# Turning the gated activation of both feed-forward networks on TensorE instead of on VectorE and ScalarE

## The reference, cut to what matters

```python
# first block
h2 = _rmsnorm(x, ffn_norm_w[l])
g, u = jnp.split(jnp.einsum('bsd,df->bsf', h2, w_gate_up[l]), 2, axis=-1)
x = x + jnp.einsum('bsf,fd->bsd', jax.nn.silu(g) * u, w_down[l])
# second block
h2 = _rms(x, g_norm2) * (1 + sc2) + sh2
gate, up = jnp.split(h2 @ w_ffn_in, 2, axis=-1)
x = x + gt2 * ((jax.nn.silu(gate) * up) @ w_ffn_out)
```

## Time and profile before

| | us |
|---|---|
| median of three runs (lowest, highest) | 2671.17 (2670.88, 2673.14) |
| the profiled execution, its own time | 2671.17 |
| its span in the trace | 2669.1 |
| TensorE busy, matmuls | 2629.4 |
| VectorE busy | 1775.1 |
| ScalarE busy | 1425.9 |

### The profile page before, as it was taken

How to read it: one execution, slowest core, us unless ns; L and a number is a source line. 1 busy time by engine, 2 the same in 40 slices (tenths; PEclk the granted TensorE clock), 3 DMA queues, 4 the chain that set the end, 5 groups by cost and what they waited for, 6 DMA issues and landing times.

```text
span 2669.1 us, 34070 instructions
## 1 busy us (share of the span) xinstructions
PE 2629.4 (99%) x12229; PEld 2188.9 (82%) x12229; DVE 1775.1 (67%) x2082; ACT 1425.9 (53%) x1844; POOL 3.2 (0%) x9
## 2 busy tenths in 40 slices
PE   8999999999999999999899999999999999999999
PEld 6888888778888888888788888888788888887887
DVE  5788677577777777888776554566577645445565
ACT  5555554456565655445556565644455555565443
POOL 0000000000000000000000000000000000000000
PEclk9999999999999999999999999999999999999999
DMA  7766555678888888888565455565578766666655
GB/s 256 241 202 197 158 143 158 214 242 278 290 276 290 276 290 271 302 281 274 175 214 179 152 166 174 152 220 187 180 248 291 250 192 191 194 189 191 203 189 173
DMA packets 306487, 583.54 MB, mean 219 GB/s; under 512 B 24095, under 2 KB 24441, under 8 KB 305865
## 3 DMA queue, kind: packets, MB, share of 16 engines
q1 hardware_dynamic: 305328, 578.45, 67.3%
q10 hardware_dynamic: 744, 2.27, 0.2%
q0 software_dynamic: 304, 1.33, 0.2%
HBM read 579.86 MB, written 2.11 MB: 218 GB/s over the span
## 4 chain that ended last, share of the span: by engine, by line
PE 92%; DVE 4%; ACT 2%; DMA 1%; issue 1%; SPq 0%; ACTq 0%; DVEq 0%
PE acc L344 29%; PE acc L346 29%; PE acc L345 29%; DVE lo L333 2%; PE ex L1031 1%; PE aux L1052 1%; PE aux L588 1%; ACT hi L327 1%; DMA raw<-w_ffn_out 1%; DMA raw<-w_proj_mla 0%; DVE op_lo L506 0%; ACT stage L491 0%; PE tp L531 0%; DVE op_hi L505 0%; PE tp L1013 0%
## 5 line engine op out<-in xcount | busy, mean ns | idle before, releaser
L333 DVE TENSOR_TENSOR lo<-raw,hi 128x1024 fp32r<-128x1024 f32 x895 | 1078.7, 1223 | 498.6 <-ACT hi L327 477.6
L327 ACT ACTIVATE hi<-raw 128x1024 fp32r<-128x1024 f32 x895 | 928.8, 1056 | 531.5 <-PE acc L346 382.7
L344 PE MATMUL acc<-hi,op_hi 128*128 128x512 f32 x2752 | 1087.5, 395 | 14.5 <-DVE lo L333 10.3
L346 PE MATMUL acc<-hi,op_lo 128*128 128x512 f32 x2752 | 1074.7, 391 | 0.0
L345 PE MATMUL acc<-lo,op_hi 128*128 128x512 f32 x2752 | 1074.1, 390 | 0.0
L344 PEld LDWEIGHTS acc<-hi,op_hi 128*128 128x128 f32 x2752 | 518.5, 188 | 126.9 <-issue 18.4
L346 PEld LDWEIGHTS acc<-hi,op_lo 128*128 128x128 f32 x2752 | 518.2, 188 | 109.6
L345 PEld LDWEIGHTS acc<-lo,op_hi 128*128 128x128 f32 x2752 | 518.9, 189 | 103.2
L344 PE MATMUL acc<-hi,f_hi 128*128 128x512 f32 x704 | 274.8, 390 | 3.7 <-DVE lo L333 3.6
L574 DVE SCALAR_TENSOR_TENSOR ada_acc<-ada_ring,cact,ada_acc 128x512 f32<-128x512 f32 x360 | 269.8, 749 | 7.3 <-DVE h_a L911 0.3
L346 PE MATMUL acc<-hi,f_lo 128*128 128x512 f32 x704 | 274.0, 389 | 0.0
(11 more groups left out here) (306 smaller groups left out, 1365.5 us busy)
## 6 DMA issues: line engine op xcount, KB each, us to landing
raw<-w_in SPq DMA_DIRECT2D x257, 512.0 KB, 3.9
ada_ring<-w_ada SPq DMA_DIRECT2D x192, 512.0 KB, 5.1
raw<-w_gate_up SPq DMA_DIRECT2D x176, 512.0 KB, 4.9
raw<-w_ffn_in SPq DMA_DIRECT2D x176, 512.0 KB, 4.5
raw<-w_down SPq DMA_DIRECT2D x88, 512.0 KB, 5.7
raw<-w_ffn_out SPq DMA_DIRECT2D x88, 512.0 KB, 4.3
raw<-w_out SPq DMA_DIRECT2D x64, 512.0 KB, 4.2
raw<-w_proj_mla SPq DMA_DIRECT2D x16, 512.0 KB, 4.2
```

What stands on the lines that cost most here:

```text
L327: A.activation(hi[:, k, :, 0:n], raw[:, k, :, 0:n], ACT.Copy).then_inc(hi_ready, 1)
L333: V.tensor_tensor(lo[:, k, :, 0:n], raw[:, k, :, 0:n], hi[:, k, :, 0:n].bitcast(F32), ALU.subtract).then_inc(lo_ready, 1)
L344: T.matmul(dst, lh, hi[:, k, kk, 0:n], start=first and kk == 0, stop=False)
L346: mm = T.matmul(dst, ll, hi[:, k, kk, 0:n], start=False, stop=last and kk == CK - 1)
```

## The change

The turn moves to TensorE. Instead of VectorE's 32 x 32 transpose there are eight transposes of 128x128 on TensorE per turn (`pe_turn`), into the two banks of `tp`; instead of ScalarE's 16 copies of 32x256 there are two of 128x512 from `tp` to `hid`, both behind its chunk (0,6). TensorE's eight stand behind its chunk (0,3) of the next pair, and for pair 10 behind the first step of `dn`. The counts of the semaphores change with it: `tr` now counts two per turn, `ev` two instead of 16, and ScalarE's silu now waits until the product before it has read `f_g`.

```diff
-        TURN = 6
-
-        def act_turn(act, n, i, part):
+        def act_turn(act, n, i):
 
             f = ff[n]
-            if part == 0:
-                act.wait_ge(f["tr"], i + 1)
-            for m in range(3 * part, min(3 * part + 3, 16)):
-                r, q = divmod(m, 4)
-                src = f_g[32 * q:32 * q + 32].rearrange("p t (c r x) -> p r c t x", c=4, r=4)[:, r]
-                dst = hid[32 * r:32 * r + 32, ds(i * 4, 4), :].rearrange("p c (t q x) -> p q c t x", t=TT, q=4)[:, q]
-                A.activation(dst, src, ACT.Copy).then_inc(f["ev"], 1)
+            act.wait_ge(f["tr"], i * 2 + 2)
+            hs = hid[:, ds(i * 4, 4), :].rearrange("p k n -> p (k n)")
+            for j in range(2):
+                A.activation(hs[:, j * NB:(j + 1) * NB], tp[:, j], ACT.Copy).then_inc(f["ev"], 1)
...
-                                act.wait_ge(f["ev"], i * 16)
+                                act.wait_ge(f["a"], i)
...
-                        if 0 <= 8 * m + k - 3 < TURN and later(i):
-                            act_turn(act, n, i - 1, 8 * m + k - 3)
+                        if m == 0 and k == 6 and later(i):
+                            evac(i - 1)
...
-                dve.wait_ge(f["tr"], i)
+                dve.wait_ge(f["tr"], i * 2)
...
-        def dve_turn(dve, n, i):
-            V.transpose(f_g[:].rearrange("p t n -> p (t n)"), f_a[:].rearrange("p t n -> p (t n)")).then_inc(ff[n]["tr"], 1)
...
-                        if m == 0 and k == 2 and later(i):
-                            dve_turn(dve, n, i - 1)
...
+        def pe_turn(pe, n, i):
+
+            f = ff[n]
+            pe.wait_ge(f["a"], i + 1)
+            if later(i):
+                pe.wait_ge(f["ev"], i * 2)
+            for j in range(2):
+                for kk in range(2):
+                    for t in range(TT):
+                        c0 = (2 * j + kk) * P
+                        ins = T.transpose(tp[:, j, kk * S + t * P:kk * S + (t + 1) * P], f_a[:, t, c0:c0 + P], ident)
+                ins.then_inc(f["tr"], 1)
...
+                    if k == 3 and later(i):
+                        pe_turn(pe, n, i - 1)
...
-                    if m == 0 and 0 <= j - 2 < TURN:
-                        act_turn(act, n, 10, j - 2)
+                    if j == 2 and m == 0:
+                        act_turn(act, n, 10)
...
-                    if j == 1 and m == 1:
-                        dve_turn(dve, n, 10)
...
+                if j == 0:
+                    pe_turn(pe, n, 10)
```

More of the change, by code:

```diff
@@ L1332, in act_gu @@
             p0 = BL[name] % 2
+            evac = lambda i: act_turn(act, n, i)
             def pair(i):
@@ L1473, in act_dn @@
                 if q == 0 and kc % 2 == 0:
-                    act.wait_ge(f["ev"], 8 * (kc + 2))
+                    act.wait_ge(f["ev"], kc + 2)
                 A.activation(f_hi[:, j % 2], hid[:, 2 * kc:2 * kc + 2, :], ACT.Copy).then_inc(f["sp"], 1)
```

## The result

The change makes the kernel slower: 2689.23 us median (2687.88 to 2690.85) against 2671.97 us, a ratio of 1.0066 with a 95% interval of 1.0054 to 1.0078 (four executions of each). On another chip it was 2688.22 against 2668.95 us, 1.0074 (1.0060 to 1.0087). The forecast was 2691.2 us, 20.0 us more than before; measured are 17.3 and 19.3 us more. The profiled execution of the changed kernel took 2690.53 us itself, 19.4 us more than that of before, and its span grew from 2669.1 to 2688.7 us.

A forecast was written before the change was run, and what follows sets the result against it. TensorE's full row was taken to bound the kernel: 2671.17 us plus 22 turns of 0.91 us (20.0 us), with nothing for removed work, new waits or remaining stalls, gave 2691.2 us, 0.75% slower; range 2689.0 to 2695.0 us.

The forecast's parts named there:

- What bounds the kernel: Whole kernel and four feed-forward stages: TensorE's row is full, busy 2629.4 of 2669.1 us, while VectorE and ScalarE have time left.
- What is removed is worth nothing: Old turn: 27.2 us of VectorE transposes and 146 us of ScalarE copies are covered by TensorE's full row.
- What the row showed: `gu1` pair of 44.47 us: 192 matmuls at 0.2267 us plus 0.95 us for L588, with nothing left over.
- The sum: TensorE's added transposes: 22 turns at 0.91 us, priced from groups L2185, make 20.0 us, between 19.6 and 20.9.
- The new waits of TensorE: Before the transposes: none, since `f_a` is ready 10 us early in `gu1` and 4 us early at `dn2`.
- The new wait of ScalarE: Copies behind chunk (0,6): hidden, 4.5 us of slack before TensorE's chunk (0,7), with 1.2 us for both copies.
- The stalls that stay: TensorE's 2.75 us wait in `dn2` for a weight load stays; counted nothing, up to 1 us either way for shifted loads.
- The range: Whole kernel time: 2689.5 to 2695.0 us as worked out, given as 2689.0 to 2695.0; the forecast has 93%.
- The closer row: 528 feed-forward chunks: less VectorE and ScalarE work closes matmul distances, kernel not slower, 2606.9 us with all 13.3 ns; chance 2%.
- ScalarE's wait: Turns in the loops: `hi` of (0,7) or a load reaches TensorE late; 1 us excess in 20 turns gives 2711 us; 4%.
- The clock: Transposes let TensorE's clock fall to 1.2 GHz for the group and a chunk: 79.9 us more, 2771 us; chance 1%.

The follow-up runs named there:

- the two halves of the change, run alone: Kernel before, old turn kept, with the eight TensorE transposes per turn added: 2688.29 us; changed kernel with its TensorE transposes left out: 2668.44 us.
- the first two experiments: TensorE's transposes added to the kernel before with its old turn kept, 1.0077; the changed kernel without its transposes, 0.9998.
- the changed kernel with the split: Changed kernel with each of the two gate-row stores issued in four parts of 512 numbers instead of at once: 2699.31 us, 1.0114.
- the split kernel: Kernel before with each of the two gate-row stores issued in four parts of 512 numbers instead of at once: 2676.73 us, 1.0029.
- the last two kernels: Kernel before with the two gate-row stores issued by GpSimd, 2672.39 us, or by ScalarE, 2673.17 us, instead of by SyncE.

## Why the prediction was right

- **What bounds the kernel.** Right. TensorE's row was full and stayed full; the two halves of the change, run alone, cost 19.6 us and -0.2 us.
- **What is removed is worth nothing.** Right, to 0.001 us of a pair's period.
- **What the row showed.** The forecast's "nothing is left over" in `gu1` proves less than it says: the 0.95 us of L588 were got as the remainder, so they had to fit. What shows it are the first two experiments. And 1188 matmuls are 6.2 pairs, not "nearly six"; the distance of 0.2267 us does not depend on it.
- **The sum.** 22 x 0.91 us. The measured price of a turn is 0.911 us in `gu1` (45.384 - 44.473) and the same in `gu2` (9.10 / 10), so 22 turns are 20.0 us. Taking the price from L2185, by distances of starts and not by durations, gave it to a hundredth of a microsecond. TensorE: Matmul & The Clock Gate, section LDWEIGHTS, in the Trainium skill gives 107 ns for a weight load of 128 columns; the kernel with doubled transposes comes close, with 109 ns from one transpose to the next (0.874 / 8). That the weight load is what sets this distance is not shown: in the trace after, a weight load of L1420 itself lasts 140 ns, overlapping its neighbours.
- **The new waits of TensorE.** None is seen, as forecast.
- **The new wait of ScalarE.** Worked out: slack 4.5 us; in the trace 4.6 us. I took 1.2 us for the copies; they take 1.09.
- **The stalls that stay.** This is the term that was mis-sized. I counted 0, with 1 us either way. In the profiled execution the wait in `dn2` was 1.03 us shorter, and one in the projection stage, which I had not listed, 0.46 us shorter: 1.5 us together. In the traces of the experiments the wait in `dn2` is anything from none (the change without its transposes) to 4.3 us (the changed kernel with the split).
- **The range.** It held by luck as well as by reason. The profiled execution, 2690.53 us, is 0.7 us under the forecast: 1.5 us less for those waits, and some 1 us more in small pieces that the ledger has outside the turns. The median of 2689.23 is lower by 1.3 us more, spread between executions that no trace explains, and lies 0.23 us inside the range; one of its four executions (2687.88) lies outside. The bounds as worked out began at 2689.5, and the measured median would have missed them; they were widened to 2689.0 without a row to support it.
- **The rivals.** The closer row: refuted by the first two experiments, since taking ScalarE's and VectorE's work away moved no distance. ScalarE's wait: not at this place, but real two chunks earlier. The clock: 1.00 in all four stages, and also with 16 transposes per turn, which cost per transpose what eight do.

## What to carry to other kernels

When one engine's row is full over whole stages, price an edit by what it adds to that row, and give nothing for what it takes off the others, however much that is (here 151 us of busy time against 20 us of elapsed). Take the price from the distance of starts around the same operation elsewhere in the trace: eight transposes of 0.27 us duration cost 0.91 us, not 2.2. And where an in-order engine waits for the full one, count the chunks queued behind the wait: the same two copies were free behind chunk (0,6) and cost 21 us behind (0,4).

## What the runs showed of the hardware that was not expected

- In a full row, a float32 transpose of 128x128 adds 0.109 us to TensorE's time where a matmul of 512 columns adds 0.227, and it makes no difference whether eight stand together or two by two (45.384 and 45.389 us per pair).
- In every trace the first weight load of 512 KB behind a store of 2048 single 4-byte numbers takes 11 to 15 us instead of the usual 4.5, whether the store is issued from SyncE's, ScalarE's or GpSimd's queue. A quarter of the numbers is no better: the store itself lands as late (9.5 to 15.7 us, where the whole one takes 12.2 to 13.1 in the kernel before), and the loads behind it take up to 12.3 us in `dn2` and up to 16.57 us in the projection stage.
- After a wait of 3.08 us in the split kernel, TensorE's granted clock stood at 0.50, the 1.2 GHz level, for six matmuls, which started 0.43 us apart instead of 0.227: some 1.2 us on top of the wait. The clock also fell behind the waits of 2.86 and 3.62 us of the last two kernels, whose matmuls start 0.43 us apart there. After the wait of 2.75 us in the kernel before it did not fall, but neither did it after the wait of 3.37 us in the projection stage of the split kernel (1.00). So the length of the wait alone does not decide.
